# Bias row of 24 modulation tiles: added by VectorE on the way out of PSUM, in place of a one-row product on TensorE

## The reference, cut to what matters

```python
def ada_params(cond, w, b):
    m = jax.nn.silu(cond) @ w + b
    return jnp.split(m[..., None, :], N_MOD, axis=-1)
```

## Time and profile before

| What | Value |
|---|---|
| Median of three runs | 4770.29 us (4761.27 to 4772.77) |
| Profiled execution, device time | 4766.14 us |
| Its span | 4764.3 us |
| TensorE (PE) busy | 3619.7 us, 76% of the span, 18771 records |
| TensorE weight loads (PEld) busy | 2098.0 us, 44% |
| VectorE (DVE) busy | 1288.0 us, 27% |
| ScalarE (ACT) busy | 802.4 us, 17% |
| GpSimd (POOL) busy | 888.8 us, 19% |
| Mean granted TensorE clock | 0.866 of full speed |
| DMA | 891.91 MB, mean 187 GB/s |

### The profile page before, as it was taken

How to read it: one execution, slowest core, us unless ns; L and a number is a source line. 1 busy time by engine, 2 the same in 40 slices (tenths; PEclk the granted TensorE clock), 3 DMA queues, 4 the chain that set the end, 5 groups by cost and what they waited for, 6 DMA issues and landing times. The chain is left out here.

```text
span 4764.3 us, 54180 instructions
## 1 busy us (share of the span) xinstructions
PE 3619.7 (76%) x18771; PEld 2098.0 (44%) x18772; DVE 1288.0 (27%) x2211; ACT 802.4 (17%) x1548; POOL 888.8 (19%) x923
## 2 busy tenths in 40 slices
PE   4989998998658887797488775976688528888881
PEld 2468966894323332333233222432444315555541
DVE  2533453443310001312100003036453321111115
ACT  1422242221011111100011111110132001111110
POOL 0034403440021111000211110033100032222223
PEclk7988998999779898897799897977689769999996
DMA  6840000002169999332599995320010129997895
GB/s 242 204 109 1 1 36 19 1 1 89 60 271 407 404 394 365 142 120 112 222 388 386 409 378 214 119 86 0 12 54 25 55 87 329 336 321 281 296 336 177
DMA packets 217938, 891.91 MB, mean 187 GB/s; under 512 B 57096, under 2 KB 57994, under 8 KB 183883
## 3 DMA queue, kind: packets, MB, share of 16 engines
q1 hardware_dynamic: 164812, 763.14, 42.8%
q10 hardware_dynamic: 30628, 76.61, 4.5%
q0 software_dynamic: 22368, 50.39, 3.4%
HBM read 831.01 MB, written 78.46 MB: 191 GB/s over the span
## 5 line engine op out<-in xcount | busy, mean ns | idle before, releaser
L1586 PE MATMUL ps<-weight_ring,moe_xT 128*64 128x256 f32 (+1 forms) x1344 | 441.0, 483 | 71.0 <-DMA weight_ring<-in_w_dram 45.1
L1586 PE MATMUL ps<-moe_spare,moe_xT 128*64 128x256 f32 (+1 forms) x1280 | 429.5, 491 | 64.1 <-issue 64.1
L1588 PE MATMUL ps<-weight_ring,moe_xT 128*64 128x256 f32 (+1 forms) x1344 | 441.4, 483 | 0.0
L1588 PE MATMUL ps<-moe_spare,moe_xT 128*64 128x256 f32 (+1 forms) x1280 | 430.4, 491 | 0.0
L1560 POOL COPY moe_xg<-moe_xin 64x1024 f32<-64x1024 f32 x168 | 173.5, 1033 | 1287.0 <-PE ps L1574 674.6
L1669 DVE TENSOR_TENSOR moe_act<-moe_sg,ps 64x256 f32<-64x256 f32 (+1 forms) x164 | 87.2, 532 | 973.2 <-ACT moe_sg L1647 973.2
L1586 PEld LDWEIGHTS ps<-weight_ring,moe_xT 128*64 128x64 f32 x1344 | 186.5, 141 | 302.5 <-issue 209.7
L1586 PEld LDWEIGHTS ps<-moe_spare,moe_xT 128*64 128x64 f32 x1280 | 179.7, 143 | 289.4 <-issue 260.0
L1672 DVE COPY moe_y<-ps 128x512 f32 x164 | 113.4, 691 | 688.0 <-PE ps L1605 503.8
L1605 PE MATMUL ps<-moe_spare,moe_aT 128*64 128x512 f32 x904 | 236.8, 660 | 25.2 <-issue 16.1
L1605 PE MATMUL ps<-weight_ring,moe_aT 128*64 128x512 f32 x944 | 232.9, 626 | 25.3 <-issue 16.6
(11 more groups left out here) (559 smaller groups left out, 5873.7 us busy)
## 6 DMA issues: line engine op xcount, KB each, us to landing
weight_ring<-in_w_dram SPq DMA_DIRECT2D x96, 2048.0 KB
moe_spare<-in_w_dram SPq DMA_DIRECT2D x96, 2048.0 KB
weight_ring<-in_w_exp_gu_dram SPq DMA_DIRECT2D x32, 2048.0 KB
moe_spare<-in_w_exp_gu_dram SPq DMA_DIRECT2D x32, 2048.0 KB
expert_rows<-moe_y ACTq DMA_DIRECT2D x328, 128.0 KB
weight_ring<-in_w_exp_dn_dram SPq DMA_DIRECT2D x16, 2048.0 KB
moe_spare<-in_w_exp_dn_dram SPq DMA_DIRECT2D x16, 2048.0 KB
expert_rows<-delta_o SPq DMA_DIRECT2D x1, 24320.0 KB, 126.5
```

The costliest lines, as they stand in the source:

```text
L1586: nc.tensor.matmul(m.ps[0:UR, 0, 0:F], xT[:, k, :], gate[:, k, :], start=(k == 0), stop=(k == KD - 1))
L1588: last = nc.tensor.matmul(m.ps[UR:P, 0, 0:F], xT[:, k, :], up[:, k, :], start=(k == 0), stop=(k == KD - 1))
```

## The change

For tiles with weights in their own buffer (`slots` above 0; 24 of the 32 tiles that `ModTiles` makes) the one-row product goes. In its place VectorE's copy out of PSUM becomes an addition, `dst = PSUM + dst`: partition 0 of `dst` holds the bias row, the other partitions must hold zeros. So GpSimd zeroes the tiles' columns at the start of each of the four stages, and the load of the bias row waits for that. The load also moves behind the loads of the first weights. TensorE no longer waits for the bias; VectorE does, ahead of its first part. `combine_stage` keeps the one-row product.

```diff
-        self.bias, self.slots = bias, slots
+        self.bias, self.slots, self.by_product = bias, slots, not slots
...
+    def zero(self, pool):
+        c0, c1 = self.tiles[0] * 512, (self.tiles[-1] + 1) * 512
+        self.nc.gpsimd.memset(self.m.mod[:, c0:c1], 0.0).then_inc(self.s.zeroed, 1)
 
     def begin(self, eng):
...
-        eng.dma_start(self.m.mod[0:1, c0:c1], self.bias[c0:c1].unsqueeze(0)).then_inc(self.s.bias_in, 16)
         for i in range(min(self.slots, self.n)):
             self.load(eng, i)
+        if not self.by_product:
+            eng.wait_ge(self.s.zeroed, 1)
+        eng.dma_start(self.m.mod[0:1, c0:c1], self.bias[c0:c1].unsqueeze(0)).then_inc(self.s.bias_in, 16)
...
             pe.wait_ge(self.s.silu, 1)
-            pe.wait_ge(self.s.bias_in, 16)
+            if self.by_product:
+                pe.wait_ge(self.s.bias_in, 16)
...
-        self.nc.tensor.matmul(ps[0:32, :], self.m.ones[0:1, 0:32], self.dst(i)[0:1, :], start=True, stop=False)
+        if self.by_product:
+            self.nc.tensor.matmul(ps[0:32, :], self.m.ones[0:1, 0:32], self.dst(i)[0:1, :], start=True, stop=False)
...
-                                             start=(x == 0 and g > 0), stop=(x == 1))
+                                             start=(x == 0 and (g > 0 or not self.by_product)), stop=(x == 1))
...
     def part_on_vector(self, dve, i):
+        if i == 0:
+            dve.wait_ge(self.s.bias_in, 16)
         dve.wait_ge(self.s.product, i + 1)
-        self.nc.vector.tensor_copy(self.dst(i), self.m.ps[:, self.banks[i % len(self.banks)], :]
-                                   ).then_inc(self.s.part, 1)
+        self.nc.vector.tensor_tensor(self.dst(i), self.m.ps[:, self.banks[i % len(self.banks)], :], self.dst(i),
+                                     ALU.add).then_inc(self.s.part, 1)
```

More of the change, by code:

```diff
@@ L220, in __init__ @@
         self.n = len(tiles)
-        self.s = st.sem("cond_in bias_in silu pick product part spread done", "mod")
+        self.s = st.sem("cond_in bias_in zeroed silu pick product part spread done", "mod")
         self.loaded = [st.sem("in_", f"mod{x}").in_ for x in range(slots)]
@@ L533, in delta_gates, with _ @@
     with st.block() as block:
+        @block.gpsimd
+        def _(pool):
+            job.zero(pool)
         @block.sync
```

## The result

The changed kernel took 4736.66 us (median of 7 runs, 4719.98 to 4743.32) against 4770.29 us (median of 7 runs, 4753.76 to 4777.80): ratio 0.9934, 95% interval 0.9914 to 0.9954. That is 33.6 us between the medians where 19.0 us were forecast, and the time lies 3.3 us under the lower end of the range. Three later comparisons of the same two kernels gave 0.9950 (0.9935 to 0.9965), 0.9953 (0.9935 to 0.9971) and 0.9949 (0.9932 to 0.9967). The four together, weighted by their intervals, are 0.9947, plus or minus 0.0009: 25 us, plus or minus 4.

A forecast was written before the change was run, and what follows sets the result against it. TensorE's own list was taken to set the pace in the four stages, except at waits for transfers. 5.8 + 7.9 + 1.9 + 3.4 = 19.0 us off 4770.3 gave 4751.3 us; range 4740 to 4766, the forecast's own 4741 to 4757.

The forecast's parts named there:

- delta_gates: Stage paced by loads: earlier releases let the last product start 2.8 to 4.1 us sooner; 3.4 taken, lower bound 1.6.
- delta_finish: Stage of two tiles: both removed products count and the wait for the second load stays; 1.9 us saved.
- convolution + next stage: Eight tiles, the fourth and last hidden behind waits for weights; six count at 0.97 us, 5.8 us saved.
- mix_columns: Stage of eight tiles: all count, since the awaited load moves up with TensorE's list; 7.9 us saved.
- The price of the one-row product: On TensorE's list, start to start: 0.97 us for each product, 1.84 us at 1.2 GHz.
- Rival 2: One-row product was hidden, other column groups running beside it, so removal gives next to nothing: 4768 us; chance 0.04.
- The additions at cost zero: VectorE's addition costs the copy's 692 ns; zeroing and later bias load delay nothing; up to 2 us in `delta_gates`.
- Rival 4: Bias row lands late in `delta_gates` or the convolution and cancels the gain, no change; chance 0.02.
- no row shows loads landing closer than 5.4 us: In `delta_gates`, the reason for capping the saving at 4.1 us: 5.4 us taken as the shortest interval between landings.
- rival 1: Longer waits in convolution and `delta_gates` put TensorE at 1.2 GHz: only 9 us gained, 4761 us; chance 0.24.
- Rival 3: TensorE's clock falls otherwise in the untouched expert stages, making the kernel slower, 4785 us; chance 0.06.
- Its sign of being wrong: In the changed kernel's profile, expert stages differing by several us from before would show the forecast wrong.

The follow-up runs named there:

- row_twice: The kernel before the change with a second one-row product, overwritten, ahead of the first in the 24 tiles; 4775.93 us, ratio 1.0037.
- row_kept: The changed kernel with a one-row product put back in the old place, its result overwritten by the products behind it; 4759.86 us, ratio 1.0002.
- gates_ahead: The changed kernel with four loads ahead in `delta_gates` instead of three, the fourth into `x_resident`; 4727.58 us, ratio 0.9941; on a second run 4733.37 us, 0.9933.
- before: The kernel without the change, in its first profile, whose execution took 4766.1 us; median of its runs 4770.29 us.
- before_again: The kernel without the change, run again unaltered for a second profile and compared with itself; 4756.68 us, ratio 0.9998.
- after: The changed kernel in its first profile, whose execution was its fastest run, 4719.98 us; median 4736.66 us, ratio 0.9934.
- again: The changed kernel, unaltered, for a second profile and comparison; 4736.89 us, ratio 0.9950.
- again2: The changed kernel, unaltered, for a third profile and comparison; 4733.82 us, ratio 0.9953.

## Why the prediction was right about the mechanism and wrong about the time

The means by stage, the old way against the new one, with the number of profiles from the table above (row_twice nowhere; for `delta_gates` without row_kept and gates_ahead):

| Term | Forecast | Old way | New way | Saved |
|---|---|---|---|---|
| `delta_gates` | 3.4 | 57.4 (3) | 50.9 (5) | 6.5 |
| `delta_finish` | 1.9 | 89.7 (4) | 87.8 (7) | 1.9 |
| convolution + next stage | 5.8 | 267.6 (4) | 263.7 (7) | 3.9 |
| `mix_columns` | 7.9 | 241.3 (4) | 231.4 (7) | 9.9 |
| sum | 19.0 | | | 22.2 |

**The price of the one-row product**, 0.97 us, held exactly, and so did the gap of 0.95 us in front of it. Rival 2, the hidden product, falls with it. row_kept and row_twice show that the product is the effect: with it back in place the gain is gone, with a second one the same amount is lost, both within some 6 us.

**The additions at cost zero** held: no wait for the bias row, 692 ns for the addition, and 1.0002 for all of them together. Rival 4 falls.

**`delta_finish`** held to 0.1 us.

**`delta_gates`** was mis-sized, 3.4 for 6.5. The step that failed here is "no row shows loads landing closer than 5.4 us". SyncE's timeline of the changed kernel, issues of the fifth and sixth loads:

```profile
115.03 0.33 SPq L246 DMA_DIRECT2D gates_mod_side<-in_ada_w_dram  x1
...
118.76 0.33 SPq L246 DMA_DIRECT2D gates_mod_side<-in_ada_w_dram  x1
```

and their times to landing:

```profile
gates_mod_side<-in_ada_w_dram SPq DMA_DIRECT2D x1, 2048.0 KB, 10.4
gates_mod_side<-in_ada_w_dram SPq DMA_DIRECT2D x1, 2048.0 KB, 11.6
```

They landed at 125.4 and 130.4, 4.9 us apart, and the fourth in time for TensorE at 120.69, 4.8 us earlier. In the earlier trace rows the queue ran out of work between loads, so their 5.4 us was no rate. A window of 13 us, from 2 to 3 us behind the issue of the fourth load, shows it in the last column (GB/s), for before:

```profile
120.00:133.00 13.00, 13.00 (x68) 3.52 (x64) 3.55 (x12) 3.70 (x7) 0.00 (x0) 0.93 0.97 376
```

and for the changed kernel:

```profile
116.30:129.30 13.00, 9.41 (x59) 2.71 (x58) 3.56 (x12) 4.05 (x8) 0.00 (x0) 1.00 1.00 429
```

2.1 MB at 429 GB/s are 4.9 us. The stage began 1.9 us earlier than before, so the last product's 130.46 is 132.3 in the old count: 5.4 us instead of 2.8 to 4.1. On average of the profiles it is 5.3 us: 2.8 for the first tile's one-row product at 1.2 GHz (1.84) and the last tile's (0.97), and 2.5 more, of which 2.2 because the fourth and the sixth load land 9.8 us apart, not 12.

The other 1.2 us stand behind the last product's start: with that product at 2.4 GHz 5.8 us are left of the stage, in four of the five profiles of the new way, and 7.3 to 7.4 with it partly or wholly at 1.2 GHz, in all three of the old way. TensorE spent 37.0 to 37.9 us of this stage at 1.2 GHz in those three and 27.3 to 30.7 in the five. How much of this follows from the shorter list and how much is chance isn't settled, and it reaches beyond the 1.2 us: row_kept, with the product in place, had 27.3 us at 1.2 GHz too. Its second tile's eight products took 1.92 us, in before 3.60; so its fifth load went out sooner, its loads also came without a gap (427 GB/s), and the stage was 3.9 us shorter than the old mean. Only the 2.8 us are surely the removed product's.

**Convolution.** 3.9 us came where 5.8 were forecast. The convolution alone became 6.2 us shorter (208.5 to 202.3), and the next stage 2.3 us longer (59.2 to 61.5). The fourth tile was hidden, as forecast. The last one was hidden by less than half: the pause ahead of the next stage's first product was 1.45 to 1.76 us in the four profiles of the old way and 1.84 to 2.31 in the seven of the new one, 0.4 us more on average, not 0.97. In two of the four the barrier ended it and not the load, as in the row below. The loss of 2.3 us is rival 1's: behind the longer wait the next stage's products ran at 1.2 GHz for longer. In before_again the first 64 records of that stage took

```profile
2145.83 27.70 PE L493 MATMUL ps<-weight_ring,yT 128*128 128x512 f32 x64 [1.45 <-PEq L184]
```

and in the changed kernel 30.44 us (the row of 2125.17 above). That stage had 0 to 3.4 us at 1.2 GHz in the four profiles of the old way, and 6.3 to 6.8 in six of the seven of the new one, 3.4 in the other. The means are 1.7 and 6.1 us; at half the clock the difference is 2.2 us lost, an estimate that matches the 2.3 us found. The Trainium skill, "TensorE: Matmul & The Clock Gate", HAM oscillation, says that waits for DMA between bursts of products put the clock back; the trace agrees at this place, behind pauses of 1.84 to 2.31 us, and the size is small, since the spell was there before in part.

**`mix_columns`.** Forecast 7.9, found 9.9. Behind the waits for the seventh and eighth loads the products ran at 1.2 GHz in before (their 16 records took 3.39 and 3.04 us) and at 2.4 GHz in after (1.92 and 1.92). The time at 1.2 GHz in the stage was 19.2 to 28.1 us the old way and 18.1 to 27.0 the new way. Half of it taken off each profile's length (an estimate: it takes TensorE as busy all that time), the stage takes 229.0 to 229.9 us the old way and 220.7 to 221.9 the new way: 8.0 us, the forecast's 7.9. So the term was right and the 2 us above it are the clock. As the times at 1.2 GHz overlap, these 2 us are not shown to be the change's.

**The step that failed for the time** is in the sum: "it lies 4.2 us below the median of the runs, which becomes 4770.3 - 19.0 = 4751.3", with "some 4 us either way for the spread of the runs". The median of three runs was taken as the level of the kernel before. Its next medians were 4757.34 (29 runs), 4754.09 (24) and 4759.74 (11), while the changed kernel's were 4736.66, 4736.89, 4733.82 and 4740.37. From the mean of those three, 4757, the forecast's 19 us lead to 4738. The range did not help: the sum's ends and the 4 us give 4744 to 4759, not the 4741 to 4757 that are written, and both are centred on the same high level. The spread has a mechanism, the granted clock. In the three later comparisons the correlation of a run's time with its mean granted clock is -0.84 (6 runs), -0.72 (7) and -0.74 (6) for the changed kernel, -0.57 (29), -0.54 (24) and -0.51 (11) for before. `again` ran between 4726.99 us at a clock of 0.874 and 4753.37 us at 0.868. In the twelve profiles everything outside the five stages of the table's first four columns takes from 4083.9 to 4114.3 us, the two ends being after and again, the same kernel. Rival 3 had the mechanism, in the scans as well as in the experts, and with no preferred sign. Its sign of being wrong, expert stages that differ by several us, came up and says nothing: the second one took 552.6 us in before and 548.2 in after, but 550.0 in before_again and 552.4 in again.

So the 46 us between the first two profiles are 24.5 us in the changed stages, 16.2 in the scans, nearly all of it the clock's, and 5.4 elsewhere, which were not taken apart. Of the 33.6 us between the first medians, 22 are the change by stages and 25 plus or minus 4 by the four comparisons. So the forecast's 19 us were 3 us low by the stages. `delta_gates` and `mix_columns` came out 3.1 and 2.0 us higher and the convolution 1.9 lower; that these errors offset each other in part is luck. Why the first seven runs of before were some 13 us slower than the later sixty-four is open: no profile exists of them but one, and it has both scans at their longest, 340 us. The three later comparisons ran on three different chips and lie within 6 us; on which chip the first one ran isn't on record. Whether a small gain of clock comes with the change beyond the stages' 22 us is open too; the comparisons allow up to 7 us.

## What to carry to other kernels

Price a removed TensorE instruction from start to start of its neighbours' weight loads, at the level of the clock that it runs at, and then look behind it for a wait for DMA that ends no earlier. That gave 7.9 us where 8.0 were found, clock aside, and failed at one place where a barrier and a load end nearly together. Where a removed instruction also releases a buffer, the next bound is the rate of the loads, and that must be read from loads that were in the queue together (4.9 us here, not 5.4). And before a change worth 0.4% is forecast as a time, ask how far apart runs of the old kernel lie: three runs don't fix its level, and one pair of profiles can show 20 us that belong to neither kernel.

## What the runs showed that was not expected

The scans have few lengths, not a continuum: of 24 scans in twelve profiles, 13 took 339.8 to 340.3 us, 7 took 336.1 to 336.6, and the rest 334.3, 334.3, 327.2 or 327.7. The time at 1.2 GHz goes with them: 68.3 us in the 340.2 us of before, 58.6 in again2's 334.25, 45 in the 327 us of after and before_again. The same instructions run each time; where the steps of the clock fall among them is decided anew in each execution. The Trainium skill, "TensorE: Matmul & The Clock Gate", What's actually happening, says that the number of slow products at a kernel's start varies from run to run. The runs here agree: 16 of TensorE's records start ahead of the first rise of the clock in before and 20 in before_again, 16 and 28 in the two profiles of gates_ahead. They also show that the same holds in the middle of a kernel and is worth 13 us in a stage of 340.
